# The projection's chunks in the recurrent rounds: two together at every second place instead of one at each of sixteen

## The reference

```python
x_mix = h[None] + xx[None] * mu[:, None, None, :]
rkv = jnp.einsum('cbsd,cde->cbse', x_mix[:3], w_rkv)     # r, k, v: 1024x1024 each
...
def step(state, inp):                                    # one token, all heads
    r_t, w_t, k_t, v_t, a_t, b_t = inp
    sa = jnp.einsum('bhij,bhj->bhi', state, a_t)
    state = (state * w_t[:, :, None, :] + sa[..., None] * b_t[:, :, None, :]
             + v_t[..., None] * k_t[:, :, None, :])
    return state, jnp.einsum('bhij,bhj->bhi', state, r_t)
...
out = ((y + bonus.reshape(B, S, D)) * g).astype(h.dtype) @ w_o
```

## Time and profile before

| | |
|---|---|
| time, median of 3 runs | 1959.42 us (1957.79 to 1961.66) |
| the profiled execution | 1955.48 us, its span 1953.7 us |
| TensorE busy | 1853.1 us, 95% of the span |
| mean granted TensorE clock | 0.981 |
| round -1 up to its last `key_norm_sum` and the wait behind it | to 148.9 us |
| rounds 0, 1, 2, 3, 4, 5, from one `key_norm_sum` to the next | 52.3, 52.9, 51.8, 52.5, 52.9, 53.2 us (starts at 143.43, 195.69, 248.56, 300.37, 352.82, 405.75, 458.99) |

### The profile page before, as it was taken

The page is one execution under the profiler, slowest core; times in us unless marked ns, Lnnn a source line. Parts: engine busy times, 40 slices in busy tenths (PEclk is TensorE's granted clock), DMA queues, the critical chain, the costliest instruction groups (busy, mean ns, idle before and its releaser), DMA issues.

```text
span 1953.7 us, 35112 instructions
## 1 busy us (share of the span) xinstructions
PE 1853.1 (95%) x15020; PEld 1425.4 (73%) x15020; DVE 946.0 (48%) x1593; ACT 781.8 (40%) x1326; POOL 205.1 (10%) x174
## 2 busy tenths in 40 slices
PE   8978999987889999999999999999999799999999
PEld 3745666655658888888887877777777588888887
DVE  6624555555535444443355545545554564444422
ACT  4333343333324222222345656566656442222211
POOL 0032333323210000000011111111111000000000
PEclk9989999998879999999999999999999899999999
DMA  3281010100213333333332222222222133333332
GB/s 119 78 262 35 17 30 29 29 27 5 70 37 94 100 95 99 95 105 91 95 99 85 69 73 76 85 68 76 76 69 72 30 101 97 97 97 97 97 97 97
DMA packets 57539, 154.95 MB, mean 79 GB/s; under 512 B 5591, under 2 KB 22535, under 8 KB 57384
## 3 DMA queue, kind: packets, MB, share of 16 engines
q1 hardware_dynamic: 57288, 152.63, 25.8%
q10 hardware_dynamic: 96, 0.07, 0.0%
HBM read 150.51 MB, written 11.61 MB: 83 GB/s over the span
## 4 chain that ended last, share of the span: by engine, by line
PE 86%; ACT 4%; DVE 4%; issue 3%; SPq 1%; DMA 1%; POOL 0%; ACTq 0%; DVEq 0%
PE bank L500 84%; PE bank L503 2%; ACT f L1415 2%; ACT f L1428 1%; SPq L459 1%; DMA f<-stream 1%; DVE f L1628 1%; SPq L442 1%; DVE f L1636 0%; ACT f L1402 0%; ACT f L1174 0%; DVE f L1511 0%; DVE f L1514 0%; DVE r L1488 0%; DVE f L1595 0%
## 5 line engine op out<-in xcount | busy, mean ns | idle before, releaser
L500 PE MATMUL bank<-r 128*128 128x512 f32 x5616 | 1304.8, 392 | 7.0 <-DVE r L1915 3.7
L500 PEld LDWEIGHTS bank<-r 128*128 128x128 f32 x5616 | 1051.0, 188 | 241.9 <-issue 18.0
L500 PE MATMUL bank<-f 64*64 64x64 f32 (+3 forms) x8940 | 503.8, 258 | 70.0 <-DVE f L1605 12.4
L500 PEld LDWEIGHTS bank<-f 64*64 64x64 f32 (+2 forms) x8940 | 321.1, 143 | 234.2 <-issue 120.9
L1488 DVE TENSOR_TENSOR r<-f,r 128x1024 fp32r<-128x1024 f32 x230 | 283.0, 1231 | 390.4 <-ACT r L1102 390.4
L1102 ACT ACTIVATE r<-f 128x1024 fp32r<-128x1024 f32 x230 | 240.7, 1047 | 153.4 <-PE bank L500 138.2
L2066 POOL TENSOR_TENSOR r<-f,r 128x512 fp32r<-128x512 f32 x48 | 62.2, 1297 | 886.1 <-ACT r L1393 886.1
L1372 ACT ACTIVATE r<-f 128x512 fp32r<-128x512 f32 x44 | 27.8, 632 | 218.1 <-DVE f L1808 218.1
L1839 DVE TENSOR_TENSOR f<-bank,f 128x512 f32<-128x512 f32 x72 | 56.0, 777 | 87.6 <-PE bank L500 84.6
L503 PEld LDWEIGHTS bank<-f 128*128 128x128 f32 x464 | 54.3, 143 | 48.6 <-ACT f L1428 26.9
L503 PE MATMUL bank<-f 128*128 128x128 f32 x464 | 70.4, 282 | 20.3 <-ACT f L1428 14.3
(11 more groups left out here) (110 smaller groups left out, 974.6 us busy)
## 6 DMA issues: line engine op xcount, KB each, us to landing
f<-stream SPq DMA_DIRECT2D x247, 512.0 KB, 3.6
bias_copies<-bias_rows SPq DMA_DIRECT2D x3, 3072.0 KB, 25.5
f<-xT SPq DMA_DIRECT2D x16, 256.0 KB, 4.1
f<-lora_out SPq DMA_DIRECT2D x16, 128.0 KB, 3.9
f<-bias_copies SPq DMA_DIRECT2D x16, 128.0 KB, 3.3
f<-bias_copies SPq DMA_DIRECT2D x32, 64.0 KB, 3.0
outT<-f SPq DMA_DIRECT2D x8, 256.0 KB, 4.5
f<-const SPq DMA_DIRECT2D x1, 576.0 KB, 3.9
```

The costliest lines, as they stand in the source:

```text
L500: return nc.tensor.matmul(out, lhsT, rhs, start=start, stop=stop, skip_group_check=True)
```

## The change

`project` does nothing at the even steps and issues two chunks at the odd ones: chunks 0 and 1 at step 1, chunks 2 and 3 at step 3, and so on. The waits of a panel's first chunk move with it, from step 0 (8) to step 1 (9). All calls stay where they are, and so does everything else on all engines; the number of instructions is the same.

```diff
             def project(k, step):
 
-                n, c = 2 * (k + 1) + step // KC, step % KC
-                if n >= N_PROJ:
+                n, late = 2 * (k + 1) + step // KC, step % KC
+                if n >= N_PROJ or late % 2 == 0:
                     return
                 p = PAN_PROJ + n
-                if c == 0:
+                if late == 1:
                     pe.wait_ge(s[f"w_raw{p % RAW}"], 16 * (p // RAW + 1))
                     if n:
                         pe.wait_ge(s["proj_sb"], n)
                 mixed = O_MIXK if n % 2 else O_MIXV
-                last = mm(banks[6][:, :], raw(p, c), f(mixed + c * S), c == 0, c == KC - 1)
-                if c == KC - 1:
+                for c in (late - 1, late):
+                    last = mm(banks[6][:, :], raw(p, c), f(mixed + c * S), c == 0, c == KC - 1)
+                if late == KC - 1:
                     last.then_inc(s["dense"], 1)
```

## The result

The changed kernel takes 1973.42 us (median of 4 runs, 1971.77 to 1975.02) beside 1959.98 us before on the same chip. The ratio is 1.0069, 95% interval 1.0052 to 1.0087: **13.5 us slower, 10.2 to 17.0**. Forecast was 13.2 us slower, 1972.6.

What follows compares the result with a forecast made beforehand. TensorE, holding 86% of the last-ending chain, was taken to bound the kernel. Round terms summed to 14.63 us, less 1.45 at the start: +13.2, 1972.6 us against the runs' median; range 1964 to 1980.

Steps and rivals of the forecast that it cites:

- The price and the floor: On TensorE: a chunk costs 0.86 us, a tile-shape change 0.20; `off_diagonal` to `next_inverse` takes at least 2.65 us.
- The 0.21 that VectorE swallows: Ahead of `a_k_v`, rounds 1 to 5: 0.21 us of the delay brought along is swallowed, counted as -0.21 each.
- the 2.6 that I named: Sign in round 3: the wait before `a_k_v` would be about 2.6 us instead of 1.75, for VectorE's L1605.
- Step 12: Around `b_scores`: -0.63 us in rounds 0 and 1, +0.43 in rounds 2 to 4, as instruction stops take back 1.06.
- the 1.5 forecast: Sign in rounds 2 to 4: the "issue" stop in `b_scores` would be about 1.5 us instead of 0.5.
- The start: Round 0: the weight wait moves from step 0 to 1; -1.45 us at half clock, -3.37 at full clock.
- the clock of these rounds is under 1.00: Sign that would make the prediction wrong: the clock of rounds 1 to 4 falling below 1.00.
- The clock rival: New waits idle TensorE; one clock fall of about 4.4 us in each of rounds 1 to 4, 1990 us; chance 0.05.
- The term of step 6: Rounds 0 to 5: the chunk leaves the wait before `a_k_v` and stands behind `mean`: +0.86 us each, +5.2 alone.
- the other terms: The change with the chunks of steps 6 and 7 left single: forecast 8.0 us slower than the kernel before.
- The faster rival: `next_inverse` follows as soon as TensorE comes, 2.2 to 2.6 us after `off_diagonal`; stops close; about 1955 us; chance 0.05.

Runs made afterwards that it cites:

- {6: 7}: Only the chunk of step 6 moved, behind that of step 7, against the kernel before: 11.6 us slower (8.6 to 14.3).
- {7: 6}: Only the chunk of step 7 moved forward to step 6, into the wait before `a_k_v`, against the kernel before: 4.1 us faster (2.2 to 5.9).
- {0: 1}: Only the chunk of step 0 moved, to step 1, with the panel's waits, against the kernel before: 2.3 us faster (0.6 to 3.9).
- the version without them in its trace: The whole change plus an extra unread matmul before `a_k_v`, against the kernel before: 12.7 us slower (9.8 to 15.4).

## Why the prediction was right

**The price and the floor** held to a hundredth: 2.66 us from `off_diagonal` to `next_inverse` at each level that the prediction named, and a pair behind it paid in full.

**`a_k_v`.** The 0.21 that VectorE swallows is there: with the chunks of steps 2, 4 and 8 moved and that of step 6 in place the wait is 1.55 instead of 1.75. That nothing is given back there is shown by {6: 7} and, from the other side, by {7: 6}. The wait after is 2.46, not the 2.6 that I named: that figure forgot the same 0.21.

**Step 12.** The stops for instructions grew as worked out, by 3 us over the rounds 2 to 4, and in the run with this step alone nothing was gained. In round 3 the stop is 1.80, above the 1.5 forecast.

**The start.** -2.3 (-3.9 to -0.6) instead of -1.45, between the bounds of half and full clock: in the trace of {0: 1} round 0 is at half clock for only a part of the pair.

**What failed** is that the clock would stay up. The prediction called itself wrong "if the clock of these rounds is under 1.00", and it is 0.97 from 155 to 440 us. Its reason was that "stretches with single waits of 1.75 kept the full clock". That came from one trace; in four others with waits of 1.75 the clock fell at 5 of 20 of them. The clock rival was priced as one long fall of 4.4 us per round, to 1990, and given 0.05. It came as short falls of about 1.35 us each, most of them at the wait before `a_k_v` that the change lengthens. The term of step 6, which I called the surest, measured 11.6 instead of 5.2 alone. In the whole change this was offset by the other terms, which measured 4.9 instead of 8.0. These two make 16.5, within 10.2 to 17.0 but above the 13.5. That the whole came so near to 13.2 is in part luck, as the falls of the clock had no place in the sum: they cost the kernel with step 6 moved several us, and the kernel without that move has fewer of them than the kernel before. At equal clock both terms come near their forecasts, by the estimate above. How much of the 13.5 is due to falls stays open: the version without them in its trace measured 12.7, which can't be told apart from it.

The faster rival is excluded: no distance from an `off_diagonal` to its `next_inverse` is under 2.65, and none of the rounds 0 to 5 of the trace got shorter.

## What to carry to other kernels

A filler on an engine that runs in order is worth what its place waits: read for each place the distance from the producer's end to the consumer's start, and take the filler from places where the next piece is ready. Before a filler is taken away from anywhere, look for the second wait that it covers by chance; here that of `output_gate` showed as a bracket of 0.57 where 0.24 is usual, and those of `variance` and `gates` came to light only without it. Merging fillers saves at most the change of tile shapes (0.20 us) at a place; here the moves of steps 4, 6, 8 and 14 each cost more than that, 0.5 to 0.9 us in a round.

## What the runs showed of the hardware

- A single wait of TensorE lengthened from 1.75 to 2.46 or 2.67 us brought the clock to half at it in 7 of 10 rounds (traces of the change and of step 6 alone, rounds 1 to 5). In five traces with the wait at 1.75 it fell there in 5 of 25, in seven with 1.55 or less in none of 35. A fall of 3.4 us cost 1.35 (3.36 us for matmuls that take 2.01 at full clock). The same wait in the same program does it in one round and not in the next.
- With a matmul of 0.86 us in the wait, whose result nobody reads, the traces of both kernels that had these falls have none from 155 to 440 us; half of the twelve runs of one of them still have a mean clock of 0.981 or less. That it pays in time is shown for none of the kernels.
- Runs of 64x64 matmuls, at 17 ns a record (127 in 2.19 us), stop for 0.2 to 1.8 us where nothing in the program is waited for, 2.3 to 2.8 us after a 16 KB transfer of instructions began (six stops of the trace after). A longer matmul taken out of such a run comes back as a longer stop: 4.1 us of stops before, 7.0 after.
